# Layer 0's first norm with four row buffers and its split on two engines, and constants ahead of the first weights

## The chip, the core and the metric

The kernel runs on one core of one Trainium2 chip. The metric is the device time of one execution in microseconds (us). TensorE is PE in the rows (its weight loads are PEld), VectorE is DVE, ScalarE is ACT, GpSimd is POOL, and SyncE, which only issues DMAs here, is SP.

## The reference, cut to what matters

One inference step of a two-layer decoder for a prompt of 1024 tokens and a sample group of 8 x 4 = 32 tokens, with D_MODEL = 1024, all in float32. Layer 0 mixes with mLSTM and retention heads, layer 1 with differential attention over a paged cache. Both begin with a root-mean-square norm and one large input projection:

```python
def rms_norm(x, g):
    xf = x.astype(F32)
    y = xf * lax.rsqrt(jnp.mean(xf * xf, axis=-1, keepdims=True) + EPS)
    return (y * g.astype(F32)).astype(x.dtype)
...
for i in range(DEPTH):
    h = rms_norm(x, norm_pre[i])
    ...                                   # layer 0: p = h @ w_in_a, conv + silu, gates, heads, w_out_a
    x = x + rms_norm(out, norm_post[i])
```

Only the norm of layer 0 and the start of its projection h @ w_in_a (1024 x 8200) are touched.

## The kernel before

The kernel is a row of stages, each a block of five engine programs that meet at a barrier: `norm_to_columns` (stage nx), `project_layer0` (p0), the gate rows and the mixing, the output projection of layer 0, the projection of layer 1, `attend`, `project_out`.

`norm_to_columns` reads the 1056 tokens in nine blocks: eight of 128 rows and the 32 sample rows. It leaves the normed activations with the model dimension on the partitions, split in two float32r parts for products near float32: h_hi is the rounded value, h_lo the rest. Two row buffers (`xb`) alternate. For each block SP loads x (L242), ACT squares it and sums along the row (L250), POOL takes mean + EPS to the power -0.5 (L268, L270), ACT scales the rows by it (L252), PE turns eight 128x128 tiles into PSUM (L288), and DVE makes h_hi as turned value times norm weight (two operations, L308) and h_lo as product minus h_hi (eight operations, L318). The norm weights were themselves turned into columns at the start (L281, L301). A row buffer is loaded again when it has been turned; a pair of PSUM banks is free again when h_lo is made. Except for the last, the blocks are in hardware loops of two.

`project_layer0` keeps the norm's result in SBUF. SP loads each head's weights in eight parts of 512 KB through two slots (`load`, L403); POOL splits each part into high and low (L650, L651) and counts qk_split or vz_split. Before the head loop PE turns the convolution's taps and the sample's convolution state (L505, L508), which wait for three loads on s_const, and multiplies the gate weights (72 matmuls, L497 to L499); ACT adds the gate bias (L574), and only then does the first tile of the first head start (L519), which also waits for four parts of qk_split. The program of each engine is written out by hand, in order; there is no planner. The start of SP's program is L461 to L472: parts 0 and 1 of the first head's weights, then gate weights, gate bias, taps, convolution bias and state, then parts 2 to 7 and the rotation tables.

Of the kernel before, what the change touches and what calls it, by code (L numbers as in the profile page):

```python
# [31 lines left out]
P = 128  # L32
D = 1024
# [175 lines left out]
def norm_to_columns(c, h_hi, h_lo):  # L209
# [3 lines left out]
    with Stage(nc, "nx") as st:  # L213
        xb = st.sb("xb", [P, 2, D])
        junk = st.sb("junk", [P, D])
        ms = st.sb("ms", [P, 2])
        rstd = st.sb("rstd", [P, 2])
        half = st.sb("half", [P, 1])
        gcol = st.sb("gcol", [P, KD])
        grow = st.sb("grow", [KD, P])  # L220
        ps = st.ps("ps", [P, 4, 512])
        psg = st.ps("psg", [P, 512])
        s_const, s_g, s_gcol = st.sem("const"), st.sem("g"), st.sem("gcol")
        loaded = st.sems("loaded", 2)
        summed, scaled, rooted, turned, taken = (st.sem(n) for n in ("summed", "scaled", "rooted", "turned", "taken"))
        act_chain, pool_chain = st.sem("act_chain"), st.sem("pool_chain")
        x_prompt = g["x_prompt"].rearrange("a (n p) d -> (a n) p d", p=P)
        x_sample = g["x_sample"].rearrange("a t d -> (a t) d")

        with nc.Block() as block:  # L230

            @block.sync
            def _(sp):
                sp.dma_start(c.ident[:], c.tab["ident"]).then_inc(s_const, 16)
                sp.dma_start(grow[:], g["norm_pre"][0, :].rearrange("(k p) -> k p", p=P)).then_inc(s_g, 16)
                for b in range(2):
                    sp.dma_start(xb[:, b, :], x_prompt[b]).then_inc(loaded[b], 16)
                with sp.Fori(1, NB // 2) as i:
                    for s in range(2):

                        sp.wait_ge(turned, 2 * i + s - 1)
                        sp.dma_start(xb[:, s, :], x_prompt[bass.ds(2 * i + s, 1)].rearrange("a p d -> (a p) d")).then_inc(loaded[s], 16)  # L242
                sp.wait_ge(turned, NB - 1)
                sp.dma_start(xb[0:S, 0, :], x_sample).then_inc(loaded[0], 16)

            @block.scalar
            def _(act):
                def one(i, s, rows):
                    act.wait_ge(loaded[s], 16 * i + 16)
                    act.activation(junk[0:rows, :], xb[0:rows, s, :], ACT.Square, accum_out=ms[0:rows, s:s + 1]).then_inc(summed, 1)  # L250
                    act.wait_ge(rooted, 2 * i + s + 1)
                    act.activation(xb[0:rows, s, :], xb[0:rows, s, :], ACT.Copy, scale=rstd[0:rows, s:s + 1]).then_inc(scaled, 1)  # L252

                with act.Fori(0, NB // 2) as i:
                    for s in range(2):
                        one(i, s, P)
                one(NB // 2, 0, S)

            @block.gpsimd
            def _(pool):  # L260
                ch = Chain(pool, pool_chain)
                ch.link(pool.memset(half[:], -0.5))
                ch.clear()

                def one(i, s, rows):

                    wait_counted(pool, summed, 2 * i + s + 1)
                    ch.link(pool.tensor_scalar(ms[0:rows, s:s + 1], ms[0:rows, s:s + 1], 1.0 / D, EPS, ALU.mult, ALU.add))  # L268
                    ch.clear()
                    pool.tensor_tensor(rstd[0:rows, s:s + 1], ms[0:rows, s:s + 1], half[0:rows, :], ALU.pow).then_inc(rooted, 1)  # L270

                with pool.Fori(0, NB // 2) as i:
                    for s in range(2):
                        one(i, s, P)
                one(NB // 2, 0, S)

            @block.tensor
            def _(pe):
                pe.wait_ge(s_const, 16)
                pe.wait_ge(s_g, 16)  # L280
                pe.transpose(psg[:, 0:KD], grow[:], c.ident[0:KD, 0:KD]).then_inc(s_gcol, 1)  # L281

                def one(i, s, rows):
                    pe.wait_ge(scaled, 2 * i + s + 1)

                    pe.wait_ge(taken, 2 * i + s + 1)
                    for k in range(KD):
                        last = pe.transpose(ps[:, 2 * s + k // 4, (k % 4) * P:(k % 4) * P + rows],  # L288
                                            xb[0:rows, s, k * P:(k + 1) * P], c.ident[0:rows, 0:rows])
                    last.then_inc(turned, 1)  # L290

                with pe.Fori(0, NB // 2) as i:
                    for s in range(2):
                        one(i, s, P)
                one(NB // 2, 0, S)

            @block.vector
            def _(dve):
                dve.sem_inc(taken, 2)
                dve.wait_ge(s_gcol, 1)  # L300
                dve.tensor_copy(gcol[:], psg[:, 0:KD]).then_inc(act_chain, 1)  # L301
                dve.wait_ge(act_chain, 1)

                def one(i, s, rows, token):
                    dve.wait_ge(turned, 2 * i + s + 1)
                    for b in range(2):
# [2485 lines left out]
```

## Time and profile before

| | |
|---|---|
| runs of the kernel | 2931.78 us median of 3 (2930.21 to 2949.38) |
| profiled execution | 2939.19 us, span 2937.1 us |
| mean granted TensorE clock | 0.953 |
| busy share of the span | PE 90%, DVE 47%, ACT 27%, POOL 13% |
| last instruction of stage nx | ends at 47.69 us |
| first instruction of stage p0 | 48.69 us |

The profiled execution is one run; its span goes from the first to the last instruction on the core. Busy shares are means over stages with different limits, so the stretches that the change touches are read by themselves. Idle time of an engine is given with what released it.

### The profile page before, as it was taken

The page shows a single profiled execution, that of the slowest core. Times are in us where ns is not written, and L with a number is a line of the kernel's source. Part 1 is how long each engine was busy: PE and PEld are TensorE (multiplying, and loading weights), DVE is VectorE, ACT ScalarE, POOL GpSimd, SP SyncE. Part 2 cuts the span into 40 slices and gives each one's busy share as a digit, 9 for nine tenths or more (in the row PEclk, how much of TensorE's full clock was granted, in tenths as well). Part 3 has the DMA queues.
Part 4 walks back from the last instruction along what each step waited for, and adds up shares of the span by engine and source line. Part 5 has one row for each costly group of instructions (what it writes and reads, how often), then busy time and mean ns, then how long its engine had stood idle before and what let it go on. Part 6 is the DMA issues. An engine that isn't in the chain of part 4 may idle for free. (4 is left out here: it accounts for less than half of the span.)

```text
span 2937.1 us, 45329 instructions
## 1 busy us (share of the span) xinstructions
PE 2634.3 (90%) x16187; PEld 1937.1 (66%) x16187; DVE 1366.1 (47%) x2413; ACT 793.0 (27%) x1981; POOL 391.7 (13%) x232
## 2 busy tenths in 40 slices
PE   4999999999964999499969999987999999999868
PEld 3888898889853777344427777764665566555556
DVE  4356554332332666412222334315766776777632
ACT  3221121111111333101111111113544555555421
POOL 3143223422300000000014123100000000000000
PEclk9999999999985999799989999997999999999979
DMA  3233223312317699642112424229999999999732
GB/s 107 83 104 96 73 82 104 97 61 82 100 41 189 185 292 283 193 166 86 47 55 79 124 80 125 65 81 351 360 371 378 363 383 382 385 373 365 261 145 98
DMA packets 323451, 535.78 MB, mean 182 GB/s; under 512 B 28525, under 2 KB 231810, under 8 KB 320042
## 3 DMA queue, kind: packets, MB, share of 16 engines
q1 hardware_dynamic: 320482, 524.66, 52.0%
q10 hardware_dynamic: 2792, 8.82, 0.8%
q8 instruction: 104, 1.70, 0.2%
q14 instruction: 73, 0.60, 0.1%
HBM read 432.06 MB, written 101.22 MB: 182 GB/s over the span
## 5 line engine op out<-in xcount | busy, mean ns | idle before, releaser
L2250 PE MATMUL at_ring<-ident,at_kp 128*128 128x128 f32 x2048 | 304.3, 282 | 23.5 <-ACT at_kT L2349 14.2
L2250 PEld LDWEIGHTS at_ring<-ident,at_kp 128*128 128x128 f32 x2048 | 226.9, 142 | 145.8 <-issue 126.9
L497 PE MATMUL p_col<-h_hi,p_wqk 128*128 128x352 f32 x768 | 248.8, 324 | 3.2 <-DVEq L675 3.2
L1884 PE MATMUL p_gm<-p_whl,h_hi 128*128 128x512 f32 (+1 forms) x576 | 229.6, 399 | 21.9 <-POOLq L1946 21.9
L499 PE MATMUL p_col<-h_hi,p_wqk 128*128 128x352 f32 x768 | 247.0, 322 | 0.0
L498 PE MATMUL p_col<-h_lo,p_wqk 128*128 128x352 f32 x768 | 246.9, 321 | 0.0
L1611 PE MATMUL oa_out<-oa_w,oa_yT 128*128 128x512 f32 x512 | 226.1, 600 | 8.4 <-ACT oa_yT L1667 5.4
L526 PE MATMUL p_row<-p_wvz,h_hi 128*128 128x512 f32 (+1 forms) x576 | 229.0, 398 | 3.5 <-ACT p_vst L600 3.5
L528 PE MATMUL p_row<-p_wvz,h_lo 128*128 128x512 f32 (+1 forms) x576 | 227.6, 395 | 0.0
L1886 PE MATMUL p_gm<-p_whl,h_lo 128*128 128x512 f32 (+1 forms) x576 | 227.2, 394 | 0.0
L527 PE MATMUL p_row<-p_wvz,h_hi 128*128 128x512 f32 (+1 forms) x576 | 227.1, 394 | 0.0
L1885 PE MATMUL p_gm<-p_whl,h_hi 128*128 128x512 f32 (+1 forms) x576 | 226.5, 393 | 0.0
L2349 ACT ACTIVATE at_kT<-at_ring 128x512 f32<-128x512 f32 x256 | 153.1, 598 | 257.5 <-PE at_ring L2250 257.5
L2471 DVE COPY at_kT<-at_ring 128x512 f32<-128x512 f32 x256 | 176.7, 690 | 74.0 <-PE at_ring L2250 42.2
L1611 PEld LDWEIGHTS oa_out<-oa_w,oa_yT 128*128 128x128 f32 x512 | 97.0, 192 | 127.2 <-issue 115.6
L497 PEld LDWEIGHTS p_col<-h_hi,p_wqk 128*128 128x128 f32 x768 | 144.6, 188 | 5.6 <-DVEq L675 3.6
L498 PEld LDWEIGHTS p_col<-h_lo,p_wqk 128*128 128x128 f32 x768 | 144.9, 189 | 0.8
L499 PEld LDWEIGHTS p_col<-h_hi,p_wqk 128*128 128x128 f32 x768 | 144.7, 188 | 0.0
L2279 PE MATMUL at_ssc<-at_kT,at_qz 128*32 128x512 f32 x1024 | 140.8, 623 | 0.0
L1884 PEld LDWEIGHTS p_gm<-p_whl,h_hi 128*128 128x128 f32 (+1 forms) x576 | 103.4, 180 | 51.3 <-POOLq L1946 22.0
L2268 PE MATMUL at_ring<-at_vp,at_aT 128*32 128x256 f32 x2048 | 123.8, 382 | 5.7 <-ACT at_kT L2349 5.0
L693 DVE TENSOR_TENSOR p_ez<-p_vst,p_ez 128x256 f32<-128x256 f32 (+1 forms) x72 | 42.6, 591 | 180.8 <-ACT p_vst L600 170.1
(341 smaller groups left out, 4386.6 us busy)
## 6 DMA issues: line engine op xcount, KB each, us to landing
at_kp<-in_cache_k SPq DMA_DIRECT2D x256, 512.0 KB, 6.3
at_vp<-in_cache_v SPq DMA_DIRECT2D x256, 512.0 KB, 6.2
p_wst<-in_w_in_a SPq DMA_DIRECT2D x64, 512.0 KB, 4.2
s_qk<-p_res SPq DMA_DIRECT2D x32, 528.0 KB, 2.8
mx_qk<-s_qk SPq DMA_DIRECT2D x16, 1024.0 KB, 10.6
p_wst<-in_w_in_c SPq DMA_DIRECT2D x64, 256.0 KB
s_v<-p_vst SPq DMA_DIRECT2D x64, 128.0 KB, 2.9
s_g<-p_gst SPq DMA_DIRECT2D x64, 128.0 KB, 2.7
```

The source lines that it names most:

```text
L497: pe.matmul(out[:, r, 0:TN], wx[:, 0, k, :], h_hi[:, k, at], start=k == 0, stop=False)
L498: pe.matmul(out[:, r, 0:TN], wx[:, 0, k, :], h_lo[:, k, at], start=False, stop=False)
L499: last = pe.matmul(out[:, r, 0:TN], wx[:, 1, k, :], h_hi[:, k, at], start=False, stop=k == KD - 1)
L526: pe.matmul(row[0:n, b % 2, :], h_hi[:, k, at], wvz[:, 0, k, :], start=k == 0, stop=False)
L527: pe.matmul(row[0:n, b % 2, :], h_hi[:, k, at], wvz[:, 1, k, :], start=False, stop=False)
L528: last = pe.matmul(row[0:n, b % 2, :], h_lo[:, k, at], wvz[:, 0, k, :], start=False, stop=k == KD - 1)
L1611: last = pe.matmul(out[s][:, f, :], yT[:, s, k, :], w[:, k, f * 512:(f + 1) * 512], start=k == 0, stop=k == KY - 1)
L1884: pe.matmul(out, c.h_hi[:, k, at_b], whl[:, s, 0, k, :], start=k == 0, stop=False)
L1885: pe.matmul(out, c.h_hi[:, k, at_b], whl[:, s, 1, k, :], start=False, stop=False)
L1886: last = pe.matmul(out, c.h_lo[:, k, at_b], whl[:, s, 0, k, :], start=False, stop=k == KD - 1)
L2250: last = pe.transpose(bank("key", n, f)[:, h * PAGE:(h + 1) * PAGE], kp[:, n % 2, k, tile:tile + P], c.ident[:])
L2471: dve.tensor_copy(kT[:, n % 2, 4:8, k * PAGE:(k + 1) * PAGE], bank("key", n, 2 * k + 1)[:].rearrange("p (h t) -> p h t", h=4)).then_inc(dv ...
```

## The change

In the norm: four row buffers in place of two, and four pairs of PSUM banks in place of two; the loops are written out; x blocks 0 and 1 are loaded first, then the norm weights, broadcast to all 128 partitions (512 KB), then the identity. DVE scales the rows by root and norm weight in one operation before the transposes, in place of ACT's scaling and the products behind them. Behind the transposes ACT writes h_hi as one rounding copy of 128x1024 and DVE writes h_lo as one subtraction. ACT and DVE take block b - 2 behind their first step for block b. In the projection the two first weight loads stand behind the constants.

```diff
--- before.py
+++ after.py
@@ -211,119 +211,106 @@
 
     nc, g = c.nc, c.x
     with Stage(nc, "nx") as st:
-        xb = st.sb("xb", [P, 2, D])
-        junk = st.sb("junk", [P, D])
-        ms = st.sb("ms", [P, 2])
-        rstd = st.sb("rstd", [P, 2])
+        x = st.sb("x", [P, 4, D])
+        junk = st.sb("junk", [P, 2, D])
+        gain = st.sb("gain", [P, D])
+        ms = st.sb("ms", [P, NB + 1])
+        rstd = st.sb("rstd", [P, NB + 1])
         half = st.sb("half", [P, 1])
-        gcol = st.sb("gcol", [P, KD])
-        grow = st.sb("grow", [KD, P])
-        ps = st.ps("ps", [P, 4, 512])
-        psg = st.ps("psg", [P, 512])
-        s_const, s_g, s_gcol = st.sem("const"), st.sem("g"), st.sem("gcol")
-        loaded = st.sems("loaded", 2)
-        summed, scaled, rooted, turned, taken = (st.sem(n) for n in ("summed", "scaled", "rooted", "turned", "taken"))
-        act_chain, pool_chain = st.sem("act_chain"), st.sem("pool_chain")
-        x_prompt = g["x_prompt"].rearrange("a (n p) d -> (a n) p d", p=P)
+        turn = [st.ps(f"turn{i}", [P, 2, 512]) for i in range(4)]
+        s_ident, s_gain = st.sem("ident"), st.sem("gain")
+        loaded = st.sems("loaded", 4)
+        summed, averaged, rooted, scaled, turned, high, low = (st.sem(n) for n in ("summed", "averaged", "rooted", "scaled", "turned", "high", "low"))
+        dve_chain, pool_chain = st.sem("dve_chain"), st.sem("pool_chain")
+        x_prompt = g["x_prompt"].rearrange("a t d -> (a t) d")
         x_sample = g["x_sample"].rearrange("a t d -> (a t) d")
+
+        def at(b):
+            return slice(b * P, b * P + rows_of(b))
+
+        def columns(b):
+            return turn[b % 4][:].rearrange("p f (k t) -> p (f k) t", t=P)[:, :, 0:rows_of(b)]
 
         with nc.Block() as block:
 
             @block.sync
             def _(sp):
-                sp.dma_start(c.ident[:], c.tab["ident"]).then_inc(s_const, 16)
-                sp.dma_start(grow[:], g["norm_pre"][0, :].rearrange("(k p) -> k p", p=P)).then_inc(s_g, 16)
-                for b in range(2):
-                    sp.dma_start(xb[:, b, :], x_prompt[b]).then_inc(loaded[b], 16)
-                with sp.Fori(1, NB // 2) as i:
-                    for s in range(2):
-
-                        sp.wait_ge(turned, 2 * i + s - 1)
-                        sp.dma_start(xb[:, s, :], x_prompt[bass.ds(2 * i + s, 1)].rearrange("a p d -> (a p) d")).then_inc(loaded[s], 16)
-                sp.wait_ge(turned, NB - 1)
-                sp.dma_start(xb[0:S, 0, :], x_sample).then_inc(loaded[0], 16)
+                def load(b):
+                    if b >= 4:
+                        sp.wait_ge(turned, b - 3)
+                    sp.dma_start(x[0:rows_of(b), b % 4, :], x_sample if b == NB else x_prompt[at(b), :]).then_inc(loaded[b % 4], 16)
+
+                load(0)
+                load(1)
+                sp.dma_start(gain[:], g["norm_pre"][0:1, :].broadcast_to([P, D])).then_inc(s_gain, 16)
+                sp.dma_start(c.ident[:], c.tab["ident"]).then_inc(s_ident, 16)
+                for b in range(2, NB + 1):
+                    load(b)
 
             @block.scalar
             def _(act):
-                def one(i, s, rows):
-                    act.wait_ge(loaded[s], 16 * i + 16)
-                    act.activation(junk[0:rows, :], xb[0:rows, s, :], ACT.Square, accum_out=ms[0:rows, s:s + 1]).then_inc(summed, 1)
-                    act.wait_ge(rooted, 2 * i + s + 1)
-                    act.activation(xb[0:rows, s, :], xb[0:rows, s, :], ACT.Copy, scale=rstd[0:rows, s:s + 1]).then_inc(scaled, 1)
-
-                with act.Fori(0, NB // 2) as i:
-                    for s in range(2):
-                        one(i, s, P)
-                one(NB // 2, 0, S)
+                def square(b):
+                    n = rows_of(b)
+                    act.wait_ge(loaded[b % 4], 16 * (b // 4 + 1))
+                    if b >= 2:
+                        act.wait_ge(summed, b - 1)
+                    act.activation(junk[0:n, b % 2, :], x[0:n, b % 4, :], ACT.Square, accum_out=ms[0:n, b:b + 1]).then_inc(summed, 1)
+
+                def take(b):
+                    act.wait_ge(turned, b + 1)
+                    act.activation(h_hi[:, :, at(b)], columns(b), ACT.Copy).then_inc(high, 1)
+
+                for b in range(NB + 1):
+                    square(b)
+                    if b >= 2:
+                        take(b - 2)
+                take(NB - 1)
+                take(NB)
 
             @block.gpsimd
             def _(pool):
                 ch = Chain(pool, pool_chain)
                 ch.link(pool.memset(half[:], -0.5))
-                ch.clear()
-
-                def one(i, s, rows):
-
-                    wait_counted(pool, summed, 2 * i + s + 1)
-                    ch.link(pool.tensor_scalar(ms[0:rows, s:s + 1], ms[0:rows, s:s + 1], 1.0 / D, EPS, ALU.mult, ALU.add))
-                    ch.clear()
-                    pool.tensor_tensor(rstd[0:rows, s:s + 1], ms[0:rows, s:s + 1], half[0:rows, :], ALU.pow).then_inc(rooted, 1)
-
-                with pool.Fori(0, NB // 2) as i:
-                    for s in range(2):
-                        one(i, s, P)
-                one(NB // 2, 0, S)
+                for b in range(NB + 1):
+                    m = ms[0:rows_of(b), b:b + 1]
+                    pool.wait_ge(summed, b + 1)
+                    ch.link(pool.tensor_scalar(m, m, 1.0 / D, EPS, ALU.mult, ALU.add))
+                    pool.tensor_tensor(rstd[0:rows_of(b), b:b + 1], m, half[0:rows_of(b), :], ALU.pow).then_inc(rooted, 1)
 
             @block.tensor
             def _(pe):
-                pe.wait_ge(s_const, 16)
-                pe.wait_ge(s_g, 16)
-                pe.transpose(psg[:, 0:KD], grow[:], c.ident[0:KD, 0:KD]).then_inc(s_gcol, 1)
-
-                def one(i, s, rows):
-                    pe.wait_ge(scaled, 2 * i + s + 1)
-
-                    pe.wait_ge(taken, 2 * i + s + 1)
+                pe.wait_ge(s_ident, 16)
+                for b in range(NB + 1):
+                    n = rows_of(b)
+                    pe.wait_ge(scaled, b + 1)
+                    if b >= 4:
+                        pe.wait_ge(low, b - 3)
                     for k in range(KD):
-                        last = pe.transpose(ps[:, 2 * s + k // 4, (k % 4) * P:(k % 4) * P + rows],
-                                            xb[0:rows, s, k * P:(k + 1) * P], c.ident[0:rows, 0:rows])
+                        last = pe.transpose(turn[b % 4][:, k // 4, (k % 4) * P:(k % 4) * P + n], x[0:n, b % 4, k * P:(k + 1) * P], c.ident[0:n, 0:n])
                     last.then_inc(turned, 1)
-
-                with pe.Fori(0, NB // 2) as i:
-                    for s in range(2):
-                        one(i, s, P)
-                one(NB // 2, 0, S)
 
             @block.vector
             def _(dve):
-                dve.sem_inc(taken, 2)
-                dve.wait_ge(s_gcol, 1)
-                dve.tensor_copy(gcol[:], psg[:, 0:KD]).then_inc(act_chain, 1)
-                dve.wait_ge(act_chain, 1)
-
-                def one(i, s, rows, token):
-                    dve.wait_ge(turned, 2 * i + s + 1)
-                    for b in range(2):
-
-                        last = dve.tensor_tensor(
-                            h_hi[:, 4 * b:4 * b + 4, token],
-                            ps[:, 2 * s + b, :].rearrange("p (k t) -> p k t", t=P)[:, :, 0:rows],
-                            gcol[:, 4 * b:4 * b + 4].unsqueeze(2).broadcast_to([P, 4, rows]), ALU.mult)
-                    last.then_inc(act_chain, 1)
-
-                    dve.wait_ge(act_chain, 2)
-                    dve.sem_clear(act_chain)
-                    dve.sem_inc(act_chain, 1)
-                    for k in range(KD):
-                        last = dve.scalar_tensor_tensor(
-                            out=h_lo[:, k, token], in0=ps[:, 2 * s + k // 4, (k % 4) * P:(k % 4) * P + rows],
-                            scalar=gcol[:, k:k + 1], in1=h_hi[:, k, token].bitcast(F32), op0=ALU.mult, op1=ALU.subtract)
-                    last.then_inc(taken, 1)
-
-                with dve.Fori(0, NB // 2) as i:
-                    for s in range(2):
-                        one(i, s, P, bass.ds(i * (2 * P) + s * P, P))
-                one(NB // 2, 0, S, slice(T, NT))
+                ch = Chain(dve, dve_chain)
+                dve.wait_ge(s_gain, 16)
+
+                def scale(b):
+                    n = rows_of(b)
+                    dve.wait_ge(rooted, b + 1)
+                    row = x[0:n, b % 4, :]
+                    dve.scalar_tensor_tensor(out=row, in0=row, scalar=rstd[0:n, b:b + 1], in1=gain[0:n, :], op0=ALU.mult, op1=ALU.mult).then_inc(scaled, 1)
+
+                def take(b):
+                    dve.wait_ge(high, b + 1)
+                    last = dve.tensor_tensor(h_lo[:, :, at(b)], columns(b), h_hi[:, :, at(b)].bitcast(F32), ALU.subtract)
+                    last.then_inc(low, 1)
+
+                for b in range(NB + 1):
+                    scale(b)
+                    if b >= 2:
+                        take(b - 2)
+                take(NB - 1)
+                take(NB)
 
 
 TN = NT // 3
@@ -458,15 +445,13 @@
                     ahead((6, 7))
                     store_rows(m, range(7, NB + 1))
 
-                load(0, 0, 0, False)
-                load(0, 0, 1, False)
                 sp.dma_start(wg[:], w[:, :, OFF_GATE:OFF_GATE + 2 * H]).then_inc(s_wg, 16)
                 sp.dma_start(gate_bias[:, 0:1], g["b_gate_i"].rearrange("a h -> h a")).then_inc(s_wg, 16)
                 sp.dma_start(gate_bias[:, 1:2], g["b_gate_f"].rearrange("a h -> h a")).then_inc(s_wg, 16)
                 sp.dma_start(tap_rows[0:CW, :], g["conv_w"][0]).then_inc(s_const, 16)
                 sp.dma_start(tap_rows[CW:CW + 1, :], g["conv_b"]).then_inc(s_const, 16)
                 sp.dma_start(buf_rows[:], g["state_mlstm_conv"].rearrange("a b r n -> (a b r) n")).then_inc(s_const, 16)
-                for part in range(2, 8):
+                for part in range(8):
                     load(0, 0, part, False)
                 sp.dma_start(cos[:], c.tab["cos0"]).then_inc(s_angles, 16)
                 sp.dma_start(sin[:], c.tab["sin0"]).then_inc(s_angles, 16)
```

## Rows read from the trace of the kernel before

**Rows 1.** Span and mean granted TensorE clock of the one core

```profile
core 0: 2937.1 us, clock 0.953
```

**Rows 2.** Busy time by stretch: us, busy us (instructions) per engine, clock, DMA

```profile
0.00:48.70 48.70, 17.04 (x73) 13.64 (x73) 29.12 (x91) 25.39 (x31) 6.96 (x23) 1.00 0.28 90
...
100.00:500.00 400.00, 400.00 (x2104) 351.04 (x2103) 220.46 (x283) 78.17 (x166) 117.46 (x64) 1.00 0.28 89
```

**Rows 3.** Timeline, first loads: start, length (us), engine, line, operation, idle before

```profile
0.75 0.41 SPq L234 DMA_DIRECT2D ident<-tab_ident  x1
...
1.63 0.83 SPq L237 DMA_DIRECT2D nx_xb<-in_x_prompt  x2
...
5.25 1.06 ACT L250 ACTIVATE nx_junk<-nx_xb 128x1024 f32<-128x1024 f32 x1 [3.08 <-DMA nx_xb<-in_x_prompt]
...
10.97 22.03 SPq L242 DMA_DIRECT2D nx_xb<-in_x_prompt  x6
```

**Rows 4.** Timeline of the norm's second loop turn, and its last h_lo

```profile
14.42 1.06 ACT L250 ACTIVATE nx_junk<-nx_xb 128x1024 f32<-128x1024 f32 x1 [1.02 <-DMA nx_xb<-in_x_prompt]
...
16.79 1.15 ACT L252 ACTIVATE nx_xb<-nx_xb,nx_rstd 128x1024 f32<-128x1024 f32 x1 [1.22 <-POOL nx_rstd L270]
...
18.00 1.97 PE L288 MATMUL nx_ps<-ident,nx_xb 128*128 128x128 f32 x8 [3.87 <-ACT nx_xb L252]
...
20.11 1.29 DVE L308 TENSOR_TENSOR h_hi<-nx_ps,nx_gcol 128x512 f32 x2 [1.82 <-PE nx_ps L288]
...
21.30 1.28 ACT L250 ACT_TABLE_LOAD   x1
...
21.66 2.16 DVE L318 SCALAR_TENSOR_TENSOR h_lo<-nx_ps,nx_gcol,h_hi 128x128 f32 x8 [0.26 <-DVEq L315]
...
23.63 1.06 ACT L250 ACTIVATE nx_junk<-nx_xb 128x1024 f32<-128x1024 f32 x1 [1.05 <-DMA nx_xb<-in_x_prompt]
...
46.33 1.36 DVE L318 SCALAR_TENSOR_TENSOR h_lo<-nx_ps,nx_gcol,h_hi 128x32 fp32r<-128x32 f32 x8 [0.18 <-DVEq L315]
```

**Rows 5.** Groups by form, last projection: count, busy us, mean ns, idle before

```profile
L2674 ACT ACTIVATE po_yT<-po_turn 128x1024 fp32r<-128x1024 f32 x8 | 8.2, 1026 | 33.1 <-DVEq L2731 27.4 <-PE po_turn L2644 5.6
...
L2715 DVE TENSOR_TENSOR po_yT<-po_turn,po_yT 128x1024 fp32r<-128x1024 f32 x8 | 9.8, 1225 | 16.7 <-ACT po_yT L2674 16.7
...
L2726 DVE SCALAR_TENSOR_TENSOR po_x<-po_out,po_ss,po_post 128x1024 f32<-128x1024 f32 x8 | 10.3, 1285 | 6.9 <-POOL po_ss L2697 6.9
```

**Rows 6.** Line 718 up to 500 us: duration ns min/median/max

```profile
L718 DVE SCALAR_TENSOR_TENSOR p_acc<-p_raw,p_taps,p_acc x48: 1283/1285/3378, 95.0 to 451.4; 128x1024 f32<-128x1024 f32 x48
```

**Rows 7.** Timeline, start of the layer-0 projection

```profile
48.69 0.94 SPq L408 DMA_DIRECT2D p_wst<-in_w_in_a  x2
...
49.68 0.50 SPq L463 DMA_DIRECT2D p_wg<-in_w_in_a  x1
...
52.18 0.30 SPq L468 DMA_DIRECT2D p_acc<-in_state_mlstm_conv  x1
...
52.76 1.04 POOL L650 CAST p_wqk<-p_wst 128x1024 fp32r<-128x1024 f32 x1 [9.85 <-DMA p_wst<-in_w_in_a]
...
56.71 1.86 PE L505 MATMUL p_row<-ident,p_raw 5*128 5x5 f32 x16 [11.51 <-DMA p_acc<-in_state_mlstm_conv]
...
65.39 2.40 POOL L651 TENSOR_TENSOR p_wqk<-p_wst,p_wqk 128x1024 fp32r<-128x1024 f32 x1
...
77.08 0.42 PE L497 MATMUL p_col<-h_hi,p_wqk 128*128 128x352 f32 x1 [3.24 <-DVEq L675]
```

**Rows 8.** Page, DMA issues: size each, median us to landing

```profile
s_g<-p_gst SPq DMA_DIRECT2D x64, 128.0 KB, 2.7
```

**Rows 9.** Line 2633, the last stage's norm weight: issue to landing

```profile
DMA to landing us min/median/max: 10.1/10.1/10.1
```

**Rows 10.** Busy time by stretch, 78 to 82 us

```profile
78.00:80.00 2.00, 2.00 (x9) 2.00 (x9) 0.00 (x0) 0.00 (x0) 1.93 (x1) 0.51 1.03 356
...
80.00:82.00 2.00, 2.00 (x10) 2.00 (x10) 0.00 (x0) 0.00 (x0) 1.58 (x2) 0.64 1.01 404
```

## The prediction

> **What bounds the kernel now.** I read the span and mean clock first [rows 1]: 2937.1 us, TensorE granted 0.953 of full speed. The same execution is timed at 2939.2 us; the median of the runs shown is 2931.8, so the profiled one stood 7.4 us above it. I make the sum against 2939.2 and carry it over to the median. Everything the change touches lies in the first 77 us: the first norm, and the order of loads at the start of the layer-0 projection. The rest runs the same instructions and can only move rigidly, or through the clock. That it moves rigidly at first is in the busy time by stretch [rows 2]: from 100 to 500 us PE is busy 400.00 of 400 us, so a projection that starts x us earlier is x us earlier at 500.
>
> In the norm's stretch no engine is busy: of 48.7 us PE works 17.0, DVE 29.1, ACT 25.4, POOL 7.0 [rows 2]. What paces it is read from the timeline of one loop turn [rows 4]. Square of block 2 starts at 14.42, the scaling copy at 16.79, eight transposes at 18.00 (until 19.97), and the next square of the same buffer only at 23.63, after a wait for the DMA. The turn is 23.63 - 14.42 = 9.2 us for two blocks: the round trip of an x buffer (square, root, scale, transposes, reload), with two buffers for it. A reload takes 14.42 - 10.97 = 3.45 us from issue to use [rows 3, 4]. Four turns and the sample block end with the last h_lo at 46.33 + 1.36 = 47.69 [rows 4].
>
> **The norm, part by part.** Four row buffers divide the 9.2 us round trip by four: 2.3 us a block, so now the engines count.
> - ACT per block: a square with its accumulator read, about 1.2 us (the scaling copy of the same size takes 1.15) and a copy of 128x1024 from PSUM, 1.03 us by the same shape in the last projection [rows 4, 5]: 2.25 us.
> - PE per block: 1.97 us, unchanged [rows 4].
> - DVE per block: removed are the two h_hi products (1.29 us) and eight small h_lo ops (2.16 us) [rows 4]; added are one scalar_tensor_tensor over 128x1024, 1.285 us by the nearest form, and one subtract of 128x1024 from PSUM, 1.225 us, the very shape of the last projection [rows 5]. With two gaps of about 0.03: 2.57, say 2.6 us. DVE becomes the bound.
> - POOL: the same two tiny ops; square start to root done stays about 2.37 us (14.42 to 16.79).
> - Queues: SP issues one DMA more per start (gain, 512 KB instead of 4 KB), and x loads 0 and 1 move ahead of both constants. Each x load now waits for the transposes of the block four back. Behind a waiting load on SP are only later loads.
>
> The order on DVE is S0 S1 S2 T0 S3 T1 ... S8 T6 T7 T8 (S scales rows, T makes h_lo); on ACT it is the same with squares and high copies. Walking it with those durations: load 0 is now issued at 0.75 in place of 1.63 [rows 3], and 5.25 - 1.63 = 3.62 us later usable: 4.4. Blocks follow at 512 KB per 1.3 us, by 404 GB/s [rows 10]: 5.8, then gain at 6.9 and the ident, blocks 2 and 3 at 8.0 and 9.4. S0 runs 6.9 to 8.2, the transposes until 10.1, ACT's high copy until 11.3, and T0 (after S2) ends at 12.9. Block 3's square waits behind that copy on ACT, so its root is there at 13.7: S3, T1 end at 16.3. Block 4's reload is issued at 10.1 and used at 13.6, its root at 15.9, before DVE is free. From 16.3 DVE doesn't idle: S4 to S8 are 5 x 1.31, T2 to T7 are 6 x 1.25, T8 (32 tokens) 0.4: 14.5 us, end 30.8. **Term 1:** 47.69 - 30.8 = **-16.9 us**. Bounds: with transposes and loads quicker everywhere (1.6 and 3.0 us) 29.3, so -18.4; with every price at its high end (S at 1.73, first load 5.2, gain at 9, reload 4.5) the same walk gives 36.4, so -11.3.
>
> The three table loads inside the loop (as at 21.30) go too. I cost them at nothing: that one ends at 22.58 and ACT still waits 1.05 us for its block [rows 4]. The Trainium skill, page "ScalarE: Activation LUTs", section "What ACT_TABLE_LOAD costs", gives about 2.66 us for a switch with its drain; by it the removed three would be worth 8.0 us more. The trace puts them beside the reload, so none of it is in the sum.
>
> **The projection's start.** Its queue begins at 48.69 (call it S) with two weight loads; the other constants are issued from 49.68, the convolution state, which PE's first work waits for, at 52.18; PE starts at 56.71 = S + 8.0, 4.5 us after that issue [rows 7]. Without the two loads ahead the state is issued 0.99 us earlier, at S + 2.5, and 1 MB (2.6 us at 404 GB/s) isn't before it. A landing of 128 KB takes 2.7 us [rows 8]; that gives S + 5.2, a gain of 2.8. If the 4.5 us stay (the many small pieces of the gate weights are the delay, not the weights), it is S + 7.0, a gain of 1.0. I take S + 5.5, **term 2: -2.5 us**, nearer the short end because a transfer of twice the data took 3.45 us alone.
>
> What is late instead: the weights, by 52.18 + 0.3 - 49.68 = 2.8 us. POOL's splits of the query/key weights start at S + 4.1 and end at 67.79 = S + 19.1 [rows 7]; they would end at S + 21.9. The first real tile starts at S + 28.4 and would at S + 25.9. So 4.0 us of cover remain, and the delay costs nothing; were the cover gone, its 2.8 us would eat term 2 whole. DVE, ACT and the gate projection between follow PE rigidly.
>
> **Sum:** -16.9 - 2.5 = -19.4 us, 2939.2 to 2919.8, and on the median 2931.8 to **2912.4 us** (-0.66%).
>
> **Rivals.**
> 1. *The scale meets POOL on DVE.* S reads two SBUF tensors; the convolution's op of that form has a median of 1.285 us and a longest of 3.378 [rows 6], and POOL is splitting weights in that stretch. Against: POOL is busy only 7.0 of 48.7 us in the norm. If S takes 1.73 (between the two, near the median) the walk ends at 33.9: 2915.5. The Trainium skill, "Advanced Engine Details and Errata", section "Mode Summary", says VectorE's second SBUF port is shared with GpSimd; the spread of that row agrees.
> 2. *The gain row is the late one.* The only broadcast of 512 KB in the trace, the last stage's norm weight, took 10.1 us to land [rows 9], though behind eight loads. At 11.7 instead of 6.9 all scales wait on DVE and the end shifts 5 us: 2917.6.
> 3. *The clock gives more.* PE's granted clock was 0.51 and 0.64 in the two slices from 78 to 82 us, just after PE had idled 3.2 us [rows 7, 10]; that cost (0.49 + 0.36) x 2 = 1.7 us. A mean of 0.953 means 0.047 x 2937 = 138 us of lost clock. If shifted timing frees a tenth of it, 2912 becomes about 2898. The transposes in the norm may also run quicker, which DVE hides but for 0.8 us.
> 4. *Slower: the clock takes more.* The same place, other sign: every stage start is a chance for a drop like that at 78, and the shift moves each of them. The whole gain is gone when 19.4 us more clock is lost, that is when the mean falls from 0.953 to 0.946; beyond that it is slower, and at 0.940 (38 us more lost) the time is 2950. For: the runs of the unchanged kernel differ. Against: nothing in the change alters PE's work after 77 us.
> 5. *It doesn't do what it says:* the in-order queues of ACT and DVE lock blocks into 3.6 us each, and the projection gains nothing. Then the norm ends near 38 and the time is 2922. Against: from block 4 on the walk has every input ready before DVE asks for it.
>
> **How the numbers follow.** The forecast 0.58, rivals in order 0.12, 0.09, 0.07, 0.05, 0.09. Range 2903 to 2924: the low end is term 1 at -18.4, term 2 at -2.8, 1.7 us of clock back (2908.9), and 6 us more for the near part of rival 3; the high end takes in rivals 1, 2 and 5 with 2 us over. A measurement of this kernel tells about 1% (29 us) from no change. Below 2902.5 lies only part of rival 3, 0.06; above 2961 only the far end of rival 4, 0.02; within, 0.92.
>
> **What will show it.** Last h_lo near 31 us; DVE without idle from about 16 us, blocks 2.6 us apart; S about 1.29 us, T 1.23; no table load after the first in the norm; first load usable near 4.4, S0 near 7. In the projection, PE's first transpose about 5.5 us after the first issue in place of 8.0, POOL's first split about 7 us after it, the first tile 25.9 us after it with POOL done 4 us before. It is wrong if squares wait for reloads in the steady part, if the first tile is released by POOL, or if the time between the first tile and the end isn't that of before.

## The result and the profile after

| | before | after |
|---|---|---|
| runs of the kernel, median | 2932.56 us of 8 (2930.21 to 2949.38) | 2913.18 us of 8 (2909.93 to 2927.41) |
| profiled execution | 2939.19 us, span 2937.1, clock 0.953 | 2913.11 us, span 2911.3, clock 0.952 |
| last h_lo of the norm ends | 47.69 us | 29.98 us |
| first issue of the projection (S) | 48.69 us | 30.75 us |
| PE's first transpose of the constants | S + 8.0 | S + 5.3 |
| first tile of the first head | 77.08 us = S + 28.4 | 56.28 us = S + 25.5 |

The ratio is 0.9928, 95% interval 0.991 to 0.9947: 19.4 us less on the medians, 0.8 us from the forecast 2912.4, and inside the 1% that the text called no change. The interval leaves out 1, so a small gain is there. In microseconds it reaches from 15.5 to 26.4, so a hit within 0.8 us is partly luck.

The first view of the kernel after is the timeline of its norm (start us, length us, engine, line, operation, idle before it and what ended that). It answers [rows 3, 4].

```profile
0.75 0.88 SPq L241 DMA_DIRECT2D nx_x<-in_x_prompt  x2
1.67 0.43 SPq L245 DMA_DIRECT2D nx_gain<-in_norm_pre  x1
...
4.57 1.06 ACT L257 ACTIVATE nx_junk<-nx_x 128x1024 f32<-128x1024 f32 x1 [2.54 <-DMA nx_x<-in_x_prompt]
...
7.49 2.48 DVE L301 SCALAR_TENSOR_TENSOR nx_x<-nx_x,nx_rstd,nx_gain 128x1024 f32<-128x1024 f32 x2 [7.49 <-DMA nx_gain<-in_norm_pre]
...
8.92 4.69 PE L289 MATMUL nx_turn<-ident,nx_x 128*128 128x128 f32 x24 [8.92 <-DVE nx_x L301]
...
11.13 1.28 DVE L301 SCALAR_TENSOR_TENSOR nx_x<-nx_x,nx_rstd,nx_gain 128x1024 f32<-128x1024 f32 x1 [1.16 <-POOL nx_rstd L278]
...
13.90 1.28 DVE L301 SCALAR_TENSOR_TENSOR nx_x<-nx_x,nx_rstd,nx_gain 128x1024 f32<-128x1024 f32 x1 [0.35 <-POOL nx_rstd L278]
...
15.24 1.09 PE L289 MATMUL nx_turn<-ident,nx_x 128*128 128x128 f32 x8 [1.63 <-DVE nx_x L301]
...
16.39 1.28 DVE L301 SCALAR_TENSOR_TENSOR nx_x<-nx_x,nx_rstd,nx_gain 128x1024 f32<-128x1024 f32 x1
17.03 1.06 ACT L257 ACTIVATE nx_junk<-nx_x 128x1024 f32<-128x1024 f32 x1 [0.68 <-DMA nx_x<-in_x_prompt]
...
17.73 1.09 PE L289 MATMUL nx_turn<-ident,nx_x 128*128 128x128 f32 x8 [1.39 <-DVE nx_x L301]
...
20.46 1.97 PE L289 MATMUL nx_turn<-ident,nx_x 128*128 128x128 f32 x8 [1.64 <-DVE nx_x L301]
...
21.46 1.27 DVE L301 SCALAR_TENSOR_TENSOR nx_x<-nx_x,nx_rstd,nx_gain 128x1024 f32<-128x1024 f32 x1
...
22.65 1.22 DVE L305 TENSOR_TENSOR h_lo<-nx_turn,h_hi 128x1024 fp32r<-128x1024 f32 x1
...
23.79 1.27 DVE L301 SCALAR_TENSOR_TENSOR nx_x<-nx_x,nx_rstd,nx_gain 128x1024 f32<-128x1024 f32 x1
...
27.31 2.67 DVE L305 TENSOR_TENSOR h_lo<-nx_turn,h_hi 128x1024 fp32r<-128x1024 f32 x3
```

Block 0 is loaded first and squared at 4.57. DVE's first scale waits for the norm weights until 7.49, those of blocks 2 and 3 (at 11.13 and 13.90) for their roots. Blocks 4 and 5 still come a little late: their squares wait 0.42 and 0.68 us for the reload (the second is the row at 17.03), and the scale of block 5 costs DVE 0.32 us of idle time. From 21.46 on DVE is the bound: scale at 21.46, h_lo at 22.65, scale at 23.79, none with an idle time behind its name. A block takes 23.79 - 21.46 = 2.33 us where it took 4.6, and the last three h_lo end at 27.31 + 2.67 = 29.98.

The projection's start, answering [rows 7]; the single rows under it are of POOL and PE alone:

```profile
30.75 0.38 SPq L448 DMA_DIRECT2D p_wg<-in_w_in_a  x1
...
32.69 0.30 SPq L453 DMA_DIRECT2D p_acc<-in_state_mlstm_conv  x1
33.11 28.50 SPq L395 DMA_DIRECT2D p_wst<-in_w_in_a  x8
...
36.09 1.86 PE L490 MATMUL p_row<-ident,p_raw 5*128 5x5 f32 x16 [7.98 <-DMA p_acc<-in_state_mlstm_conv]
37.66 1.04 POOL L635 CAST p_wqk<-p_wst 128x1024 fp32r<-128x1024 f32 x1 [11.93 <-DMA p_wst<-in_w_in_a]
```

```profile
50.41 2.40 POOL L636 TENSOR_TENSOR p_wqk<-p_wst,p_wqk 128x1024 fp32r<-128x1024 f32 x1
```

```profile
56.28 0.42 PE L482 MATMUL p_col<-h_hi,p_wqk 128*128 128x352 f32 x1 [3.25 <-DVEq L660]
```

The gate weights are issued first, the convolution state 1.94 us later, the weight parts behind it. PE starts at S + 5.34. POOL's first split is late (S + 6.9, forecast about 7), its last for the query and key weights ends at 52.81 = S + 22.1, and the first tile still comes 3.5 us behind that, released by DVE as before.

### The profile page after: what moved, and what is told of

Its sections match the earlier page's. It is cut to its first block and busy times, and to the rows that moved or that the text cites. A ratio compares the mean times of both kernels' runs of the same rounds, so it can differ in the third digit from the quotient of the medians.

```text
span 2911.3 us, 45047 instructions
## 1 busy us (share of the span) xinstructions
PE 2619.7 (90%) x16186; PEld 1934.3 (66%) x16186; DVE 1357.1 (47%) x2340; ACT 785.9 (27%) x1978; POOL 392.6 (13%) x232
```

## The experiments

Where no label of its own says more, an experiment is one edit of the kernel before or of the one after. All stage times are of one profile each; the norm's end is that of the last h_lo. How much one profile tells: the norm of the kernel before ends at 47.69, 47.93 and 48.11 us in three of them, the norm of the change at 29.63 to 30.72 in seven. Runs of the kernel before stood beside each group, with medians of 2934.9, 2931.1 and 2932.0 us.

| kernel | norm's end | first tile | time, median us | ratio to before |
|---|---|---|---|---|
| before | 47.69 | 77.08 | 2932.6 | |
| before, loops written out (e5) | 46.47 | 75.56 | 2941.2, one run | |
| + four buffers, old operations (e4) | 41.35 | 70.24 | 2927.3 | 0.9975 (0.9956 to 0.9993) |
| new operations, two buffers (e3) | 49.57 | 76.16 | 2931.5 | 0.9982 (0.9964 to 1.0) |
| after | 29.98 | 56.28 | 2913.2 | 0.9928 (0.991 to 0.9947) |
| after, on another chip | 30.37 | 56.83 | 2911.9 | 0.9929 (0.9903 to 0.9954) |

**Two buffers with the new operations.** In `norm_to_columns`:

```diff
-        x = st.sb("x", [P, 4, D])
+        x = st.sb("x", [P, 2, D])
-        turn = [st.ps(f"turn{i}", [P, 2, 512]) for i in range(4)]
+        turn = [st.ps(f"turn{i}", [P, 2, 512]) for i in range(2)]
...
-                    if b >= 4:
-                        sp.wait_ge(turned, b - 3)
+                    if b >= 2:
+                        sp.wait_ge(turned, b - 1)
```

> The changed kernel with two row buffers and two pairs of banks in place of four; operations, engines and load order as changed. Theory (the reload round trip bounds two buffers, whatever the operations are): the walk with its durations gives the last h_lo at about 47 us, so nearly all of the 17.7 us is lost and the time is some 17 us over the changed kernel's. Rival (the cheaper operations are the gain, the buffers only help): the end stays under 38 us.

Its timeline: two squares of the same buffer, the transposes between them, and the last h_lo.

```profile
14.04 1.06 ACT L257 ACTIVATE nx_junk<-nx_x 128x1024 f32<-128x1024 f32 x1 [7.09 <-DMA nx_x<-in_x_prompt]
...
24.18 1.06 ACT L257 ACTIVATE nx_junk<-nx_x 128x1024 f32<-128x1024 f32 x1 [5.51 <-DMA nx_x<-in_x_prompt]
```

```profile
18.70 1.94 PE L289 MATMUL nx_turn<-ident,nx_x 128*128 128x128 f32 x8 [6.54 <-DVE h_lo L305]
```

```profile
49.15 0.42 DVE L305 TENSOR_TENSOR h_lo<-nx_turn,h_hi 128x256 fp32r<-128x256 f32 x1 [0.50 <-ACT h_hi L261]
```

A turn of two blocks takes 24.18 - 14.04 = 10.1 us and the norm ends at 49.57, later than in the kernel before. The buffer's round trip bounds it. The reload is 3.5 us of that (from 18.70 + 1.94 = 20.64 to 24.18), and the new order adds to the rest: the transposes wait for a pair of banks, which is free when h_lo of the block two back is made, and on DVE that h_lo stands behind the scale of the very block that is to be turned. The theory holds, by 2.6 us more than its walk gave. In this order, and with two pairs of banks, the new operations bring nothing. Row buffers and banks were always changed together here, so which of the two is needed isn't shown, nor what another order would do with two.

**Four buffers with the old operations.**

```diff
-        xb = st.sb("xb", [P, 2, D])
+        xb = st.sb("xb", [P, 4, D])
-        ps = st.ps("ps", [P, 4, 512])
-        psg = st.ps("psg", [P, 512])
+        ps = st.ps("ps", [P, 8, 512])
+        psg = ps[:, 7, :]
...
-                with dve.Fori(0, NB // 2) as i:
...
+                for b in range(NB + 1):
+                    one(b, b % 4, rows_of(b), slice(b * P, b * P + rows_of(b)))
```

> The kernel before with four row buffers and four pairs of banks, loops written out, its old operations on DVE (two products, eight small h_lo operations) and ACT's scaling copy in its old place. Theory (with the buffers there, DVE's 1.29 + 0.28 + 2.16 us a block bound it at about 3.7 us, against ACT's square, root and copy in series at 3.5): last h_lo near 42 to 43 us, so buffers alone bring about 5 of the 17.7 us and the split on whole blocks the other 12. Rival (buffers are the gain): end at 32 or less.

```profile
17.66 1.28 DVE L298 TENSOR_TENSOR h_hi<-nx_ps,nx_gcol 128x512 fp32r<-128x512 f32 x2
...
21.20 1.28 DVE L298 TENSOR_TENSOR h_hi<-nx_ps,nx_gcol 128x512 fp32r<-128x512 f32 x2
```

```profile
39.99 1.36 DVE L308 SCALAR_TENSOR_TENSOR h_lo<-nx_ps,nx_gcol,h_hi 128x32 fp32r<-128x32 f32 x8 [0.18 <-DVEq L305]
```

DVE's products of two blocks lie 21.20 - 17.66 = 3.54 us apart, with h_lo between them and no idle time of DVE but 0.2 us before h_lo, for its own product: it is the bound, and the norm ends at 41.35, a little before the 42 to 43 expected. Buffers and banks without the rest bring 5.1 us over the written-out loops (46.47 to 41.35), the new operations, with their order and the order of the first loads, another 11.4.

**Loops written out, nothing else.** The edit is the one of the loops above with two buffers.

> The kernel before with its norm loops written out and nothing else, so that the table loads inside the loop go. Theory (they run beside the reload): last h_lo at 46.5 to 47.7 us, at most 1 us for the loop's own registers and branches. Rival, by the rule that each table load holds ACT about 2.7 us: 8 us sooner, near 40.

```profile
14.21 1.06 ACT L245 ACTIVATE nx_junk<-nx_xb 128x1024 f32<-128x1024 f32 x1 [2.30 <-DMA nx_xb<-in_x_prompt]
...
23.07 1.06 ACT L245 ACTIVATE nx_junk<-nx_xb 128x1024 f32<-128x1024 f32 x1 [2.31 <-DMA nx_xb<-in_x_prompt]
```

```profile
45.11 1.36 DVE L307 SCALAR_TENSOR_TENSOR h_lo<-nx_ps,nx_gcol,h_hi 128x32 fp32r<-128x32 f32 x8 [0.18 <-DVEq L304]
```

The table load between the turns is gone, and the square's wait for its block has grown from 1.05 us [rows 4] to 2.31. The turn is 23.07 - 14.21 = 8.86 us against 9.21; these 0.35 us are of the loops' own instructions or of the table loads, which the edit doesn't separate. The norm ends 1.2 us sooner, not 8: the loads of the table were hidden, as costed. So here the 2.66 us that the Trainium skill gives for a switch (page "ScalarE: Activation LUTs", section "What ACT_TABLE_LOAD costs") aren't a price of the path. The single time of 2941.2 us is long because of the attention stage, shown at the end.

**The norm weight left out of the scale.** DVE scales by the root alone, from one tensor; the outputs lack the norm weight of layer 0.

```diff
-                    dve.scalar_tensor_tensor(out=row, in0=row, scalar=rstd[0:n, b:b + 1], in1=gain[0:n, :], op0=ALU.mult, op1=ALU.mult).then_inc(scaled, 1)
+                    dve.tensor_scalar(row, row, rstd[0:n, b:b + 1], None, ALU.mult).then_inc(scaled, 1)
```

> The changed kernel with the norm weight left out: DVE scales the rows by the root alone, one source tensor in place of two (the weight row is still loaded and waited for). Theory (DVE at 2.5 us a block is the bound): the scale drops to about 0.7 us, ACT's 2.25 us and the reload become the bound, last h_lo near 28.7 in place of 30.0. Rival (the round trip of four buffers or ACT is the bound already): 29.8 or later.

```profile
20.02 0.75 DVE L301 TENSOR_SCALAR nx_x<-nx_x,nx_rstd 128x1024 f32<-128x1024 f32 x1
20.18 1.06 ACT L257 ACTIVATE nx_junk<-nx_x 128x1024 f32<-128x1024 f32 x1 [0.19 <-DMA nx_x<-in_x_prompt]
20.69 1.22 DVE L305 TENSOR_TENSOR h_lo<-nx_turn,h_hi 128x1024 fp32r<-128x1024 f32 x1
...
24.87 2.84 DVE L305 TENSOR_TENSOR h_lo<-nx_turn,h_hi 128x1024 fp32r<-128x1024 f32 x3
```

The scale takes 0.75 us in place of 1.27, the norm ends at 27.71, 2.3 us sooner (1.3 were expected), and the one execution took 2908.3 us. DVE was the bound of the steady part. Half a microsecond a block over nine blocks would be 4.7; the rest isn't got because the other engines come next (at 20.18 ACT waits for a block).

**Weights ahead of the constants again.** The changed kernel with the second part of the change undone, first in one execution (2912.95 us), then in twelve.

```diff
+                load(0, 0, 0, False)
+                load(0, 0, 1, False)
                 sp.dma_start(wg[:], ...).then_inc(s_wg, 16)
...
-                for part in range(8):
+                for part in range(2, 8):
```

> The changed kernel with one thing put back: the first two weight loads of the projection stand ahead of the constants again. Forecast's theory (the megabyte ahead delays the constants): the time from the stage's first issue to PE's first transpose goes from 5.3 back to 8.0 us, POOL's first split comes at 4.1 us instead of 6.9, the first tile at 28.4 instead of 25.5; norm's end unchanged at 30.0. Rival (the 2.7 us came from something else, for instance a shorter landing by chance): 5.3 us stay.

```profile
30.60 0.93 SPq L395 DMA_DIRECT2D p_wst<-in_w_in_a  x2
...
34.60 1.04 POOL L637 CAST p_wqk<-p_wst 128x1024 fp32r<-128x1024 f32 x1 [9.09 <-DMA p_wst<-in_w_in_a]
...
38.58 1.86 PE L492 MATMUL p_row<-ident,p_raw 5*128 5x5 f32 x16 [10.70 <-DMA p_acc<-in_state_mlstm_conv]
```

```profile
59.38 0.42 PE L484 MATMUL p_col<-h_hi,p_wqk 128*128 128x352 f32 x1 [3.25 <-DVEq L662]
```

S is 30.60. POOL splits at S + 4.0, PE starts at S + 8.0 and the first tile comes at S + 28.8: term 2 is undone, 3.3 us at the tile. The one execution took no longer than the changed kernel, so whether the delay arrives at the end needs more of them:

> The changed kernel with the first two weight loads ahead of the constants again, now timed: the single look had its first tile 28.9 us after the stage's first issue, 3.3 us later than the changed kernel. Theory: 2914 to 2915 us, the changed kernel's 2912 and those 3 us. Rival: absorbed, 2912.

2916.15 us over 12 runs (0.9955, 0.9938 to 0.9973), against 2911.9 and 2913.2 of the changed kernel: 3.0 and 4.2 us later, though the intervals overlap. Part of it is a matter of shares: five of these 12 runs lie at 2923 to 2930 us, three of the changed kernel's 14 at 2923 to 2927, which looks like the long attention stage shown at the end. The medians of the others are 2914.3 and 2911.2, 3.1 us apart, as the theory has it. The traces agree. In the second profile the first tile comes at S + 28.2 (S + 25.7 in the changed kernel's second), so undoing costs 2.5 to 3.3 us there; and the stage behind the projection starts at 841.4 us in both, against 838.4 and 839.2. The other way round, the same edit in the kernel before:

> The kernel before with one edit of the change alone: the projection's constants ahead of its first weight loads, old norm. Theory: norm's end stays at 47.7 us, the first tile comes 25.5 us after the stage's first issue in place of 28.4, and 2.5 to 3 us arrive at the end of the kernel (2928 to 2929 against 2931). Rival: they are absorbed later in the projection (a weight part that is late), and the time is that of before.

Its norm ended at 48.11 and its first tile came at 75.05, S + 26.0, not quite the S + 25.5 expected. The time is 2931.1 against 2932.0, ratio 0.9992 (0.9977 to 1.0007): the 2.5 to 3 us expected aren't in the run times, and by these alone it is inconclusive. The traces have them for two thirds of the kernel: the attention stage starts at 1979.5 us, against 1982.5 and 1982.6 in two profiles of the kernel before. Behind that point this profile has the longest attention stage of all, 827.0 us.

**Towards a better version.** Two edits follow from the profile after. One loads the constants and the first two weight parts at the end of SP's program in the norm, into tensors of the projection allocated before it:

```diff
             @block.sync
             def _(sp):
...
                 for b in range(2, NB + 1):
                     load(b)
+                ahead(sp)     # gate weights, biases, taps, state, weight parts 0 and 1
```

> The changed kernel, with the projection's constants and its first two weight parts loaded at the end of SP's program in the norm, into tensors of the projection that are allocated before the norm. Theory (the 5.3 us between stage start and PE's first transpose are all transfer): PE starts within 0.6 us of the stage, the first tile at 20.8 us after its start instead of 25.5, total 4 to 5 us less. Rival (POOL's splits or the memset and split of the gate weights become the wait): less than 2 us. Rival on the other side: the loads disturb the norm's last x block, and its end moves past 30.5.

```profile
30.45 1.83 PE L508 MATMUL p_row<-ident,p_raw 5*128 5x5 f32 x16 [2.31 <-PEq L179]
...
51.12 0.42 PE L500 MATMUL p_col<-h_hi,p_wqk 128*128 128x352 f32 x1 [3.25 <-DVEq L678]
```

The stage starts at 30.4; PE works at 30.45 and the first tile comes at 51.12, 20.7 us after the stage's start; the norm's end is 29.63, undisturbed. 2906.57 us (0.9901, 0.9878 to 0.9925), 5.3 under the changed kernel on the same chip. The other edit, on top of the first, lets the gate projection write the second accumulator, so that the first tile needn't wait until ACT has read the gates:

```diff
-                columns(col[0][0:32 + H], wg_hl[:]).then_inc(s_gate, 1)
-
-                pe.wait_ge(s_tr2, 4)
+                columns(col[1][0:32 + H], wg_hl[:]).then_inc(s_gate, 1)
...
+                dve.sem_inc(tile_taken, 1)
                 dve.wait_ge(s_tr2, 4)
                 ch.link(dve.memset(raw[:, :, 0:NR], 0.0))
-                dve.sem_inc(tile_taken, 2)
+                dve.sem_inc(tile_taken, 1)
```

> As the one with the prefetch, and the gate projection goes to the second accumulator, so that the first tile doesn't wait for ACT to read the gates. Theory (PE idles 3.2 us there and then runs at the half level for about 3.5 us): another 3.3 us for the idle time and up to 1.7 us of clock, so 8 to 10 us less than the changed kernel in all. Rival: the first tile is then released by POOL's splits, and only part of it comes.

```profile
48.95 0.32 PE L500 MATMUL p_col<-h_hi,p_wqk 128*128 128x352 f32 x1
```

The first tile now has no idle time before it, and the granted clock stays at 1.00 over the next 4 us, where it was 0.59 in the changed kernel. The norm ended at 30.72 in this profile, past the 30.5 that the expectation of the prefetch named as a disturbance; the one above and the spread of the seven speak against it. 2902.53 us (0.9896, 0.9871 to 0.9921): 9.4 us under the changed kernel, 28.6 under the one before, and the lowest median, though its interval overlaps that of the prefetch alone. The bank alone, without the prefetch:

> The changed kernel with the gate projection in the second accumulator, without the prefetch. Theory (the wait for ACT's read of the gates and the drop of the clock behind it): with the prefetch the first tile came 3.2 us sooner against the stage's start than without this edit; here POOL's splits end 19.7 us after the stage's first issue and the gate projection ends near 22.3, so the same 3.2 us come: 2908 to 2909 us. Rival: POOL is late and releases the first tile.

```profile
53.08 0.42 PE L482 MATMUL p_col<-h_hi,p_wqk 128*128 128x352 f32 x1 [0.37 <-POOLq L635]
```

2908.03 us (0.9917, 0.9892 to 0.9942), 4 to 5 us under the changed kernel. The first tile comes at S + 22.3, 3.3 us sooner, and the clock's drop behind it is gone too (1.00 over the next 4 us). Here the rival is right about the releaser: the first tile waits for POOL's split, 0.37 us. With the weights behind the constants that cover is used up, and only with the prefetch is there room again.

**The changed kernel beside them, and the kernel before once more.**

> The changed kernel itself again, on the same chip as the two versions beside it: 2913 us, ratio to the kernel before 0.993.

2911.91 us of 6 runs, 0.9929.

> The kernel before, a second profile. The profiled pair differs by 26 us, the medians by 19; 7.7 of the 26 lie in the attention stage (818.8 against 811.1 us), which the change doesn't touch. Theory (that stage has executions with more and with fewer stretches at half clock, whatever the kernel; more likely now the fewer): the stage takes 811 to 812 us here, or again 819 to 827, and all stages but it and the mixing agree with the first profile within 2 us. Rival (the change's shift in time frees the stage): 818 or more, as in the first profile, and never 811 for this kernel.

The attention stage from its first to the next stage's first instruction, PE alone, in the kernel before, the same kernel again, the changed one, and the best version (length, PE busy, clock, DMA share, GB/s):

```profile
1982.50:2801.20 818.70, 748.24 (x6840) 0.96 0.95 356
```

```profile
1982.60:2794.50 811.90, 742.02 (x6840) 0.97 0.95 359
```

```profile
1964.90:2776.00 811.10, 742.28 (x6840) 0.97 0.95 360
```

```profile
1953.80:2777.10 823.30, 753.66 (x6840) 0.95 0.95 355
```

The two profiles of the kernel before differ by 6.9 us of span (2937.1 and 2930.2), and by 818.7 - 811.9 = 6.8 in this stage. The changed kernel shows 811.1, its sibling with two more edits 823.3. So the 26 us between the first pair of profiles hold 7 that come and go in the kernel before by itself; its second profile against the one after gives 18.9.

## Why the prediction was right

**The norm, term 1** (-16.9): measured -17.7 us. The walk said DVE bounds it with 1.285 and 1.225 us an operation; the rows after have 1.27 to 1.28 and 1.22. The first scale came 0.6 us later than the walk's 6.9 (x 0, x 1, the norm weights and the identity are in flight together), but that cost nothing, because DVE waited for the roots of blocks 2 and 3 anyway: the scale of block 4 starts at 16.39, and the walk had 16.3. The 0.8 us lie behind that point. Successive DVE operations start 1.13 to 1.20 us apart though each lasts 1.22 to 1.27, so they overlap by some 0.08 where I had put gaps of 0.03, and a block took 2.33 us in place of 2.6. "From block 4 on every input is ready" was slightly too good: blocks 4 and 5 waited for their reloads, which the text had named as a sign of being wrong, and it cost DVE 0.3 us. That both halves are needed wasn't in the prediction's sum as such: written-out loops give 1.2 us, buffers and banks on top of them 5.1, the rest 11.4, and the rest with two buffers -1.9 (49.57 against 47.69).

**Table loads at nothing:** right, shown by the loops written out.

**The projection's start, term 2** (-2.5): measured -2.7 at PE's first transpose and -2.9 at the first tile; undone it is 2.5 to 3.3 at the tile. The megabyte ahead was the delay. Inside the term two sizes were off and nearly cancelled: the state was issued at S + 1.94 and not at S + 2.5, and was used 36.09 - 32.69 = 3.4 us later, not 2.7. (The reload that the text called twice the data of the 128 KB landing is 512 KB, four times; the sum doesn't hang on it.) The late weights cost nothing, with 3.5 us of cover left against the 4.0 expected. The last experiments show how thin that cover is.

**The rest moves rigidly:** nearly, and by differences that cancel. The first tile came 20.8 us sooner in the first pair of profiles and 20.4 in the second, the median 19.4. The lengths of the stages behind the tile, in us:

| | before | before, again | after | after, on another chip |
|---|---|---|---|---|
| projection behind the first tile | 784.1 | 784.3 | 782.1 | 782.4 |
| mixing | 342.9 | 342.6 | 346.0 | 342.4 |
| from there to the attention stage | 743.5 | 743.5 | 745.4 | 745.5 |
| attention | 818.8 | 811.9 | 811.1 | 811.4 |

The second and fourth rows differ within one kernel. The first and third repeat, with opposite signs, and the prediction had neither. The first can be placed. At 551 us of the kernel before, 474 behind the first tile, PE waits for ACT and ACT for a store (its issue on SP takes 0.82 us, and 0.33 at the same place after), and the granted clock drops behind that wait. Before, then after, each with PE's wait and the stretch behind it:

```profile
550.98 0.50 PE L526 MATMUL p_row<-p_wvz,h_hi 128*128 128x512 f32 x1 [1.84 <-ACT p_vst L600]
```

```profile
552.00:556.00 4.00, 4.00 (x12) 0.57 0.59 204
```

```profile
529.53 0.50 PE L511 MATMUL p_row<-p_wvz,h_hi 128*128 128x512 f32 x1 [1.06 <-ACT p_vst L585]
```

```profile
530.00:534.00 4.00, 4.00 (x19) 1.00 0.83 264
```

That wait is 1.84 to 1.89 us in the three profiles whose norm has hardware loops (in one of them, with the constants first, the clock's drop doesn't follow) and 0.93 to 1.16 in the eleven with the loops written out, the one that changes nothing else among them. So these 2 us go with the written-out loops and thus with the change, though not with its argument. Why the store is later isn't shown, and the 2 us that are lost again before the attention stage aren't explained.

**The rivals.** The scale took 1.28 us while POOL worked beside it, but POOL's operations there are of one element a row; beside its large ones it wasn't measured. The norm weights were a little late (0.6 us, not 5). Lock-step of the queues appears only with two buffers. Neither clock rival came: the means are 0.953 and 0.952, and 0.001 of them is 3 us.

## What to carry to other kernels

A stage in which no engine is busy for two thirds of the time is read by the round trip of one of its buffers; more buffers pay only down to the busiest engine's time per block, so cut that time in the same change. Count what each engine does per block before and after: here 5.1 us came from the buffers and banks, 11.4 from the operations that these had laid open. At a stage boundary, look which load the first instruction waits for and what is queued ahead of it, and then whether it could be issued in the stage before.

## What the runs showed of the hardware

PE's two clock levels (1.2 and 2.4 GHz) in the norm: the transposes of a 128-row block took 1.97 us in every block of before ([rows 4] show one), each transpose 421 ns. After, the first 16 took the same, then came three blocks at the upper level with 273 ns a transpose (1.14 us from 12.47 on, then 1.09 twice), and then 1.97 again. The stretches of those transposes, PE alone (busy us, instructions, granted clock, DMA share, GB/s):

```profile
8.00:12.00 4.00, 3.08 (x15) 1.00 0.44 176
12.00:16.00 4.00, 2.37 (x18) 1.00 0.85 269
16.00:20.00 4.00, 1.43 (x12) 0.93 0.74 261
20.00:24.00 4.00, 3.18 (x14) 0.50 0.05 17
24.00:28.00 4.00, 2.96 (x20) 0.72 0.00 0
```

PE had worked from 8.92 to 13.61 almost without a pause and was at the upper level from 12.5 us on. The granted clock reads 1.00 before and behind that point, as it does over the whole norm of before with its 421 ns [rows 2], so here only the lengths tell the level: I take 421 ns for the lower one, because a transpose takes 417 ns where the granted clock reads 0.50. From 14 to 20 us PE was busy with two short blocks, 1.09 us each, and from 20 to 24 the granted clock was 0.50. DVE hid both. The drop at 78 us of the kernel before [rows 10] came back in the changed one 20 us sooner, behind the same idle time of PE, and was gone in the two versions without that idle time.

The attention stage is the larger surprise: 809 to 813 us at a mean clock of 0.97, or 819 to 827 at 0.95 to 0.96, whichever kernel it was (both for the kernel before). The five profiles with the long stage are those timed at 2939.2, 2941.2 and 2945.4 us, where the kernel before has a median of 2932, and those of the prefetch without and with the other bank, 2917.3 and 2915.2 us over medians of 2906.6 and 2902.5. What decides between the two isn't known.
